# A two-layer decoder trunk on one Trainium2 core: the attention core with stationary values, sparse branches summed in PSUM, and probabilities scaled on VectorE

## The chip, the cores and the metric

The kernel runs on one of the eight cores of one Trainium2 chip. The metric is the device time of one execution in microseconds. Three runs of the kernel before gave 1229.21, 1229.42 and 1230.17 us, so the median is 1229.42 us.

## The reference

The input is one sequence of 256 positions with 1024 channels. Two layers follow each other; the change touches only the attention mixer of the first. Its 8 sparse heads (in 2 groups of 4, which share keys and values) have three branches, each a softmax of its own, combined by sigmoid gates; its 8 "fox" heads have one causal softmax with a bias from a cumulative log forget gate. With 256 positions every block of the selected branch and the whole window are seen, so both are plain causal attention, on their own keys and values.

```python
# sparse heads: three branches per head, each masked_softmax(q k^T * scale) v
o_c = einsum('bgrqn,bngd->bqgrd', p_c, v_cmp)      # 15 compressed blocks
o_s = einsum('bgrqk,bgqkd->bqgrd', p_s, vg)        # selected blocks
o_w = einsum('bgrqk,bkgd->bqgrd', p_w, vw)         # window
o_a = gates[..., 0:1] * o_c + gates[..., 1:2] * o_s + gates[..., 2:3] * o_w
# fox heads
s_f = q k^T * scale + cq[..., None] - cum_t[:, :, None, :]
o_b = einsum('bhqk,bkhd->bqhd', masked_softmax(s_f, causal), vb)
x = x + concatenate([o_a, o_b]) @ w_out
```

After it come a dense SwiGLU, a gated linear attention layer and a mixture of 8 SwiGLU experts. They make up most of the time and are the same in both kernels.

## The kernel before, in words

The program is written by hand, engine by engine: for each engine one function lists its instructions in order, and semaphores (`S["probs"]` and so on) carry what one engine waits for from another. Nothing schedules it: an engine takes its instructions in the written order, and one that waits holds all that stand behind it on that engine.

Weights stream from HBM in units of 1 MB into a ring of eight buffers; ScalarE (ACT in the rows) rounds each unit into a high part (`split`, L1197) and VectorE (DVE) forms the low part (L1577). A product of activations and weights is three matmuls (L562 to L564), high by high, high by low, low by high.

The stage in question stands between the input projection and the output projection. It has 18 units: a unit is one branch (0 selected, 1 window, 2 fox), one tile `t` of 128 queries, and `n` heads, 4 heads with 128 keys each where t is 0, 2 heads with 256 keys each where t is 1. So a unit's scores always fill a PSUM bank of 512 columns. Two units, one of each group of heads, make a pair; there are 9 pairs. For a unit:

1. TensorE (PE) computes the scores of a pair (`qk_pair`, L765) and adds the mask with a matmul against an identity (L768).
2. DVE takes the row maximum from PSUM and multiplies it by minus the scale (`rowmax`, L1830 and L1831).
3. ACT computes the exponentials, head by head, with their row sums (L1327), into `pbuf`, which has two buffers.
4. PE turns the probabilities, four 128x128 transposes (`turn`, L778).
5. DVE copies the turned probabilities from PSUM into `ptb` (L1859).
6. PE multiplies them with the values (`pv`, L796): the turned probabilities are the stationary side (128x128), the values of one head the moving side (64 columns). The result has queries on partitions. Each product of two f32 matrices shows as two matmul records.

After the last unit of each branch and tile DVE runs `take`: reciprocal of the sums (L1838), times the gate (L1843), the product with the branch's output from PSUM (L1844) and the sum into `hn` (L1845), for fox only L1838 and L1840. The compressed branch is one matmul for each tile (L803), its output scaled into `hn` at L1851. The order on PE is: scores of pair p+1, then for both units `turn(u)`, `pv(u-1)`. At the end `hn` is turned for the output projection (L572, 8 transposes for tile 0 before the projection, 8 for tile 1 after its first 12 matmuls), and ACT (L1206) and DVE (L1588) split it into high and low part. Just ahead of the stage DVE does the softmax of the compressed branch (L1805 to L1809), a weight split (L1577) and copies (L1816, L1820).

## Time and profile before

| what | us |
|---|---|
| median of three runs (lowest, highest) | 1229.42 (1229.21, 1230.17) |
| span of the profiled execution, first to last instruction | 1227.6 |
| attention stage in it (first scores to first matmul of the output projection) | 84.72 to 128.17, 43.45 long |
| busy in the whole span: PE, DVE, ACT | 1213.1, 977.8, 815.7 |
| busy in the stage: PE, DVE, ACT | 42.71, 36.55, 22.92 |

The profiled execution has no time of its own in the list beside its span; the median of the runs is 1.8 us above the span. Times in rows are in microseconds from the start of the span; "PEld" is the load of a stationary operand and overlaps the matmuls. A matmul's row says first the stationary shape (contraction * columns), then the output's. The duration of a matmul overlaps the next one's, so that the distance of starts tells its cost.

### The profile page before, as it was taken

Reading aid. Unit: us, or ns where it says so; the run is one execution under the profiler, and the core shown is the slowest. Engines: PE = TensorE matmul, PEld = TensorE weight load, DVE = VectorE, ACT = ScalarE, POOL = GpSimd, SP = SyncE. Lnnn points to the kernel's source line nnn. Section 1 sums busy time; section 2 is a strip of 40 time slices with the busy share of each in tenths; the row PEclk is TensorE's granted clock in tenths of the full one; section 3 lists DMA queues with packets and bytes.
Section 4 is the critical chain, followed back from the end, with each engine's and each line's share of the span. In section 5 each row is a group of like instructions: output and inputs, shape, how many; then the busy total and the mean of one; then the engine's idle time right before and its main releaser. Section 6 shows DMA issues by size and latency. Waiting matters only on the chain.

```text
span 1227.6 us, 16109 instructions
## 1 busy us (share of the span) xinstructions
PE 1213.1 (99%) x5992; PEld 1009.8 (82%) x5992; DVE 977.8 (80%) x959; ACT 815.7 (66%) x877; POOL 35.5 (3%) x41
## 2 busy tenths in 40 slices
PE   8999999999999999999999999999999999999997
PEld 6878888888898888888888888888888888888886
DVE  6998564554557478999989989889889889889896
ACT  7765354344375467777777777777777777777773
POOL 0000000000000001100000000000000000000300
PEclk9999999999999999999999999999999999999999
DMA  9730254455534256999999999999999999999992
GB/s 352 306 137 2 102 192 170 170 188 206 206 138 141 101 192 236 392 397 369 413 367 370 407 370 375 408 365 373 407 368 376 399 372 374 392 364 376 399 421 85
DMA packets 53000, 361.42 MB, mean 294 GB/s; under 512 B 6048, under 2 KB 6560, under 8 KB 10944
## 3 DMA queue, kind: packets, MB, share of 16 engines
q1 hardware_dynamic: 49872, 349.41, 73.8%
q0 software_dynamic: 3056, 11.02, 2.3%
q8 instruction: 50, 0.82, 0.3%
q14 instruction: 22, 0.18, 0.0%
HBM read 354.63 MB, written 5.77 MB: 294 GB/s over the span
## 4 chain that ended last, share of the span: by engine, by line
PE 96%; DVE 1%; ACT 1%; DMA 1%; SPq 0%; issue 0%; DVEq 0%
PE bank L562 29%; PE bank L564 29%; PE bank L563 29%; PE bank L1105 2%; PE bank L796 1%; PE bank L952 1%; PE bank L765 1%; DMA raw<-in_weights 1%; PE bank L572 1%; PE bank L1070 0%; PE bank L778 0%; PE bank L840 0%; ACT hT_hi L1212 0%; PE bank L1062 0%; PE bank L973 0%
## 5 line engine op out<-in xcount | busy, mean ns | idle before, releaser
L2174 DVE TENSOR_TENSOR low<-raw,whi 128x2048 fp32r<-128x2048 f32 x260 | 594.9, 2291 | 66.3 <-ACT whi L1508 59.0
L1508 ACT CAST whi<-raw 128x2048 fp32r<-128x2048 f32 x260 | 497.2, 1912 | 112.3 <-PE bank L564 111.6
L562 PE MATMUL bank<-whi,hT_hi 128*128 128x512 f32 (+1 forms) x1104 | 430.6, 390 | 0.8 <-DVE low L1660 0.5
L564 PE MATMUL bank<-whi,hT_lo 128*128 128x512 f32 (+1 forms) x1104 | 428.7, 388 | 0.0
L563 PE MATMUL bank<-low,hT_hi 128*128 128x512 f32 (+1 forms) x1104 | 428.0, 388 | 0.0
L562 PEld LDWEIGHTS bank<-whi,hT_hi 128*128 128x128 f32 x1104 | 207.4, 188 | 43.4 <-DVE hT_lo L1595 0.9
L564 PEld LDWEIGHTS bank<-whi,hT_lo 128*128 128x128 f32 x1104 | 207.3, 188 | 42.7
L563 PEld LDWEIGHTS bank<-low,hT_hi 128*128 128x128 f32 x1104 | 207.4, 188 | 41.7
L1577 DVE TENSOR_TENSOR low<-raw,whi 128x2048 fp32r<-128x2048 f32 x67 | 152.9, 2288 | 45.0 <-ACT whi L1197 44.9
L562 PE MATMUL bank<-whi,h_hi 128*128 128x512 f32 x440 | 181.0, 411 | 0.0
L564 PE MATMUL bank<-whi,h_lo 128*128 128x512 f32 x440 | 172.5, 392 | 0.0
L563 PE MATMUL bank<-low,h_hi 128*128 128x512 f32 x440 | 172.1, 391 | 0.0
L1197 ACT CAST whi<-raw 128x2048 fp32r<-128x2048 f32 x67 | 128.1, 1918 | 8.2 <-PE bank L564 5.4
L564 PEld LDWEIGHTS bank<-whi,h_lo 128*128 128x128 f32 x440 | 82.6, 188 | 17.9
L563 PEld LDWEIGHTS bank<-low,h_hi 128*128 128x128 f32 x440 | 83.1, 189 | 14.2
L562 PEld LDWEIGHTS bank<-whi,h_hi 128*128 128x128 f32 x440 | 82.7, 188 | 13.7
L1525 ACT ACTIVATE sg<-bank 128x256 f32<-128x256 f32 x88 | 33.9, 385 | 65.2 <-PE bank L564 65.2
L1350 ACT ACTIVATE sg<-bank,rstd 128x256 f32<-128x256 f32 x22 | 10.5, 475 | 98.4 <-PE bank L564 98.3
L1887 DVE SCALAR_TENSOR_TENSOR hact<-bank,rstd,sg 128x256 f32<-128x256 f32 x22 | 10.6, 484 | 57.6 <-ACT sg L1350 57.6
L2179 DVE TENSOR_TENSOR h_lo<-bank,h_hi 128x256 fp32r<-128x256 f32 x88 | 36.8, 418 | 1.0 <-ACT h_hi L1512 1.0
L2191 DVE TENSOR_TENSOR hact<-sg,bank 128x256 f32<-128x256 f32 x88 | 36.4, 414 | 0.0
L1512 ACT CAST h_hi<-bank 128x256 fp32r<-128x256 f32 x88 | 32.8, 373 | 2.8 <-PE bank L1105 2.8
(318 smaller groups left out, 779.4 us busy)
## 6 DMA issues: line engine op xcount, KB each, us to landing
raw<-in_weights SPq DMA_DIRECT2D x327, 1024.0 KB, 5.7
sums<-ybuf POOLq DMA_DIRECT2D x7, 512.0 KB, 6.8
arena<-in_compress SPq DMA_DIRECT2D x1, 1088.0 KB, 15.8
x<-in_x SPq DMA_DIRECT2D x2, 512.0 KB, 5.4
raw<-in_weights SPq DMA_DIRECT2D x4, 256.0 KB, 6.1
raw<-in_weights SPq DMA_DIRECT2D x2, 512.0 KB, 8.0
tokens<-hng POOLq DMA_DIRECT2D x2, 512.0 KB, 8.6
out<-x SPq DMA_DIRECT2D x4, 256.0 KB, 2.7
```

Of the source, the lines that this page charges most:

```text
L562: mm(out_, a_hi, b_hi, start=start, stop=False)
L563: mm(out_, a_hi, b_lo, start=False, stop=False)
L564: return mm(out_, a_lo, b_hi, start=False, stop=stop)
L1105: last = nc.tensor.transpose(bank[2][:, j * P:(j + 1) * P], hact[:, (par + c) % 2, j * P:(j + 1) * P], ident)
L1197: nc.scalar.copy(whi[:, u % SPLIT, :, :], raw[:, u % RAW, :, :]).then_inc(S["w_hi"], 1)
L1508: nc.scalar.copy(whi[:, u % SPLIT, :, :], raw[:, u % RAW, :, :]).then_inc(S["w_hi"], 1)
L1512: nc.scalar.copy(h2_hi[:, (par + c) % 2, :], bank[2][:, 0:CH]).then_inc(S["m_h2_hi"], 1)
L1525: A(sg[:, (par + c) % 2, :], bank[(par + c) % 2][:, 0:CH], ACT.Silu).then_inc(S["m_silu"], 1)
L1577: V.tensor_tensor(low[:, u % RAW, :, :], raw[:, u % RAW, :, :], whi[:, u % SPLIT, :, :].bitcast(F32), ALU.subtract).then_inc(S["w_lo"], 1)
L2174: V.tensor_tensor(low[:, u % RAW, :, :], raw[:, u % RAW, :, :], whi[:, u % SPLIT, :, :].bitcast(F32), ALU.subtract).then_inc(S["w_lo"], 1)
L2179: V.tensor_tensor(h2_lo[:, (par + c) % 2, :], bank[2][:, 0:CH], h2_hi[:, (par + c) % 2, :].bitcast(F32), ALU.subtract).then_inc(S["m_h2T"], 1)
L2191: V.tensor_tensor(hact[:, (par + c) % 2, :], sg[:, (par + c) % 2, :], bank[(par + c) % 2][:, CH:2 * CH], ALU.mult).then_inc(S["m_hact"], 1)
```

## The change

- The values become the stationary side of the product of probabilities and values, and the turned probabilities the moving side: 128x64 stationary, up to 512 moving columns. The output has channels on partitions (64 for each half) and queries along the columns, which is the layout in which the output projection reads it. The two groups of sparse heads (or an even and an odd fox head) write the lower and the upper 64 partitions of the same bank.
- The compressed, selected and window branches of the sparse heads accumulate in one PSUM bank for each tile, so the probabilities must be normalised and gated first: `scaled` on DVE takes the reciprocal of the sums and multiplies each head's probabilities in `pbuf` (now four buffers) by reciprocal and gate, in place, before `turn`.
- `take`, the scaling into `hn`, and the 16 transposes of `hn` are gone. `heads_out` (ACT) and `heads_lower` (DVE) read the output banks directly. The rows of the output weights are permuted on the host (`heads_paired`).
- Queries are stored times minus the scale, masks are +1e30, and the row minimum takes the place of the maximum, so that it is the bias as it stands and L1831 is gone.
- The compressed branch's probabilities are multiplied by their factors before they are turned; its product is four matmuls for each tile.
- The order of pairs and of instructions is another: selected and window of tile 0, then of tile 1, then fox; scores run two pairs ahead.

```diff
+        att_pairs = [(br, 0, 0, 4) for br in range(2)] + [(br, 1, h0, 2) for br in range(2) for h0 in (0, 2)]
+        att_pairs += [(2, 0, 0, 4), (2, 1, 0, 2), (2, 1, 2, 2)]
+        att_units = [(br, t, h0 + 4 * g, n) for br, t, h0, n in att_pairs for g in range(NG)]
...
             def turn(u):
-                pe.wait_ge(S["probs"], u + 1)
+                br, t, h0, n = att_units[u]
+                pe.wait_ge(S["scaled"], u + 1)
...
+            def blocks_out(t):
+                for r in range(4):
+                    c = slice(r * P, (r + 1) * P)
+                    mm(bank[4 + t][:, c], vbd[:, c], pcT[:, t, :], start=(r == 0), stop=False)
+            def pv(p):
+                br, t, h0, n = att_pairs[p]
+                out_ = bank[4 + t]
+                pe.wait_ge(S["probsT"], 2 * p + 2)
+                if br == 2 and h0 == 0:
+                    pe.wait_ge(S["hT"], turned_at(1, t, 0))
+                for kt_ in range(t + 1):
+                    if br < 2:
+                        for g in range(NG):
+                            v = proj[1][:, kt_, br * P + g * HD:br * P + (g + 1) * HD]
+                            last = mm(out_[g * HD:(g + 1) * HD, h0 * P:(h0 + n) * P], v,
+                                      ptb[:, g, kt_ * n * P:(kt_ + 1) * n * P], start=False,
+                                      stop=(br == 1 and h0 + n == 4 and kt_ == t))
+                        continue
+                    for g, j in product(range(NG), range(n)):
+                        h, m = h0 + 4 * g + j, kt_ * n + j
+                        half, c = h % 2 * HD, slice(h // 2 * P, (h // 2 + 1) * P)
+                        last = mm(out_[half:half + HD, c], proj[5][:, kt_, h * HD:(h + 1) * HD],
+                                  ptb[:, g, m * P:(m + 1) * P], start=(kt_ == 0 and h < 2),
+                                  stop=(kt_ == t and h >= 6))
             qk_pair(0)
             pe.wait_ge(S["cmp_pT"], 1)
             for t in range(NT):
-                mm(bank[4 + t][:, :], pcT[:, t, :], vbd, start=True, stop=True).then_inc(S["cmp_o"], 1)
-            for u in range(AU):
-                if u % 2 == 0 and u + 2 < AU:
-                    qk_pair(u + 2)
-                turn(u)
-                if u == AU - 2:
-                    transposes(hn, 1, 0, lambda half: pe.wait_ge(S["o_done"], 7))
-                if u >= 1:
-                    pv(u - 1)
-            pv(AU - 1)
-            by_tile(U_A_OUT, 0, A_OUT_BANKS[0], 1, (0, 4),
-                    lambda: transposes(hn, 1, 1, lambda half: pe.wait_ge(S["o_done"], 8)))
+                blocks_out(t)
+            qk_pair(1)
+            for p in range(AP):
+                turn(2 * p)
+                turn(2 * p + 1)
+                if p + 2 < AP:
+                    qk_pair(p + 2)
+                if p + 1 < AP:
+                    pv(p)
+            by_tile(U_A_OUT, 0, A_OUT_BANKS[0], 1, (0, 4), lambda: pv(AP - 1))
...
-                if u >= 2:
-                    act.wait_ge(S["probsT_psum"], u - 1)
+                if u >= 4:
+                    act.wait_ge(S["probsT_psum"], u - 3)
...
-            V.tensor_tensor(s16, s16, bc(cm01, 2, NH), ALU.mult).then_inc(S["cmp_p"], 1)
+            V.tensor_tensor(s16, s16, bc(cm01, 2, NH), ALU.mult)
...
+            V.tensor_tensor(s16, s16, bc(f3, 3, 16), ALU.mult).then_inc(S["cmp_p"], 1)
             split(14)
...
+            def scaled(u):
+                br, t, h0, n = att_units[u]
+                dve.wait_ge(S["probs"], u + 1)
+                link(V.reciprocal(fac[:, seq_of(u), h0:h0 + n], sums[:, seq_of(u), h0:h0 + n]))
+                kw = (t + 1) * P
+                for h in range(h0, h0 + n):
+                    p_ = pbuf[:, u % 4, (h - h0) * kw:(h - h0 + 1) * kw]
+                    last = V.tensor_scalar(p_, p_, fac[:, seq_of(u), h:h + 1],
+                                           gates[:, t, h, br + 1:br + 2] if br < 2 else 1.0, ALU.mult, ALU.mult)
+                last.then_inc(S["scaled"], 1)
...
+            for u in range(4):
+                row_least(u)
+            scaled(0)
+            scaled(1)
+            for p in range(AP):
+                for u in (2 * p, 2 * p + 1):
+                    probs_turned(u)
+                    if p + 1 < AP:
+                        scaled(u + 2)
+                if p + 2 < AP:
+                    row_least(2 * p + 4)
+                    row_least(2 * p + 5)
+                if p == 3:
+                    heads_lower(0, 0)
+                if p == 6:
+                    heads_lower(1, 0)
+            heads_lower(0, 1)
+            heads_lower(1, 1)
```

Three places show how instructions move. On PE, a pair of tile 1 in the steady part of the stage. Before (bank0 and bank1 take scores, bank2 and bank3 turned probabilities, bank4 and bank5 outputs):

```order
L765 MATMUL bank1<-arena 128x256
L768 MATMUL bank0<-msk_bits 128x2x128
L768 MATMUL bank1<-msk_bits 128x2x128
L778 MATMUL bank2<-cst,arena 128x128 [waits probsT,probs]
L778 MATMUL bank2<-cst,arena 128x128 x3
L796 MATMUL bank4<-arena 128x64 [waits probsT]
L796 MATMUL bank4<-arena 128x64 x3
L778 MATMUL bank3<-cst,arena 128x128 [waits probsT,probs]
L778 MATMUL bank3<-cst,arena 128x128 x3
L796 MATMUL bank5<-arena 128x64 [waits o_done,probsT]
L796 MATMUL bank5<-arena 128x64 x3
```

In the changed kernel (L764 and L767 are scores and mask, L781 the transposes, L802 the product with the values; 64x256 is the output):

```order
L781 MATMUL bank2<-cst,arena 128x128 [waits probsT,scaled]
L781 MATMUL bank2<-cst,arena 128x128 x3
L781 MATMUL bank3<-cst,arena 128x128 [waits probsT,scaled]
L781 MATMUL bank3<-cst,arena 128x128 x3
L764 MATMUL bank6<-arena 128x256 [waits probs]
L764 MATMUL bank7<-arena 128x256
L764 MATMUL bank6<-arena 128x256
L764 MATMUL bank7<-arena 128x256
L767 MATMUL bank6<-msk_bits 128x2x128
L767 MATMUL bank7<-msk_bits 128x2x128
L802 MATMUL bank5<-arena 64x256 [waits probsT]
L802 MATMUL bank5<-arena 64x256 x3
```

Eight products a pair became four, both transposes stand together ahead of the scores, and they wait for `scaled` instead of `probs`.

On DVE, the head of the stage. Before:

```order
L1830 TENSOR_REDUCE arena<-bank0 128x4 [waits scores,dve_chain]
L1831 TENSOR_SCALAR arena<-arena 128x4 [waits dve_chain]
L1830 TENSOR_REDUCE arena<-bank1 128x4 [waits scores]
L1851 TENSOR_TENSOR hn<-bank4,arena 128x512 [waits cmp_o]
L1851 TENSOR_TENSOR hn<-bank5,arena 128x512 [waits cmp_o]
L1830 TENSOR_REDUCE arena<-bank6 128x2 [waits scores]
L1831 TENSOR_SCALAR arena<-arena 128x2 [waits dve_chain]
L1859 COPY arena<-bank2 128x512 [waits probsT_psum]
```

In the changed kernel (L1859 is now the row minimum, L1868 and L1872 are `scaled`, L1881 the copy of turned probabilities):

```order
L1859 TENSOR_REDUCE arena<-bank0 128x4 [waits scores]
L1859 TENSOR_REDUCE arena<-bank1 128x4 [waits scores]
L1859 TENSOR_REDUCE arena<-bank6 128x4 [waits scores]
L1859 TENSOR_REDUCE arena<-bank7 128x4 [waits scores]
L1868 RECIPROCAL arena<-arena 128x4 [waits probs]
L1872 TENSOR_SCALAR arena<-arena 128x128 [waits dve_chain]
L1872 TENSOR_SCALAR arena<-arena 128x128 x3
L1881 COPY arena<-bank2 128x512 [waits probsT_psum]
```

The minima of the second pair now stand ahead of the first scaling, and two scalings ahead of the first copy.

On DVE, one pair of tile 1 in the steady part. Before, with a `take` in it:

```order
L1830 TENSOR_REDUCE arena<-bank0 128x2 [waits scores]
L1831 TENSOR_SCALAR arena<-arena 128x2 [waits dve_chain]
L1859 COPY arena<-bank2 128x512 [waits pv,probsT_psum]
L1838 RECIPROCAL arena<-arena 128x8 [waits pv]
L1843 TENSOR_TENSOR arena<-arena 128x8 [waits dve_chain]
L1844 TENSOR_TENSOR arena<-bank4,arena 128x512 [waits dve_chain]
L1845 TENSOR_TENSOR hn<-hn,arena 128x512 [waits dve_chain]
L1830 TENSOR_REDUCE arena<-bank1 128x2 [waits scores]
L1831 TENSOR_SCALAR arena<-arena 128x2 [waits dve_chain]
L1859 COPY arena<-bank3 128x512 [waits pv,probsT_psum]
```

In the changed kernel:

```order
L1881 COPY arena<-bank2 128x512 [waits pv,probsT_psum]
L1868 RECIPROCAL arena<-arena 128x2 [waits probs]
L1872 TENSOR_SCALAR arena<-arena 128x256 [waits dve_chain]
L1872 TENSOR_SCALAR arena<-arena 128x256
L1881 COPY arena<-bank3 128x512 [waits pv,probsT_psum]
L1868 RECIPROCAL arena<-arena 128x2 [waits probs]
L1872 TENSOR_SCALAR arena<-arena 128x256 [waits dve_chain]
L1872 TENSOR_SCALAR arena<-arena 128x256
L1859 TENSOR_REDUCE arena<-bank6 128x2 [waits scores]
L1859 TENSOR_REDUCE arena<-bank7 128x2 [waits scores]
```

The four instructions of `take`, once for each branch and tile, are gone; a reciprocal and two (tile 0: four) multiplications stand in every unit.

## Rows read from the trace of the kernel before

**Rows 1.** The page: busy time by engine, us (share) and count.

```profile
PE 1213.1 (99%) x5992; PEld 1009.8 (82%) x5992; DVE 977.8 (80%) x959; ACT 815.7 (66%) x877; POOL 35.5 (3%) x41
...
PE 96%; DVE 1%; ACT 1%; DMA 1%; SPq 0%; issue 0%; DVEq 0%
```

**Rows 2.** Busy time by stretch, attention stage: length, engines, granted clock, DMA.

```profile
84.72:128.17 43.45, 42.71 (x344) 36.42 (x343) 36.55 (x79) 22.92 (x100) 0.00 (x0) 1.00 0.06 23
```

**Rows 3.** Groups by form, same stage: count | busy, mean ns | idle before.

```profile
L796 PE MATMUL bank<-arena 128*128 128x64 f32 x144 | 18.9, 274 | 0.7 <-DVE arena L1859 0.6
```

**Rows 4.** Timeline, PE, 104 to 112 us: start, us, engine, line, operation.

```profile
105.14 1.14 PE L765 MATMUL bank<-arena 64*128 64x256 f32 x8
106.20 0.39 PE L768 MATMUL bank<-msk_bits 128*128 128x256 bf16 x2
106.43 0.60 PE L778 MATMUL bank<-cst,arena 128*128 128x128 f32 x4
107.28 1.10 PE L796 MATMUL bank<-arena 128*128 128x64 f32 x8 [0.24 <-DVE arena L1859]
108.22 0.61 PE L778 MATMUL bank<-cst,arena 128*128 128x128 f32 x4
108.68 1.10 PE L796 MATMUL bank<-arena 128*128 128x64 f32 x8
109.62 2.00 PE L765 MATMUL bank<-arena 66*128 66x128 f32 x16
```

**Rows 5.** Timeline, PE, 84.5 to 90 us, the stage's head.

```profile
84.72 1.16 PE L765 MATMUL bank<-arena 64*128 64x128 f32 x16
...
86.39 1.98 PE L803 MATMUL bank<-arena 128*128 128x512 f32 x4
88.30 1.14 PE L765 MATMUL bank<-arena 64*128 64x256 f32 x8
```

**Rows 6.** Timeline, VectorE, 81 to 86.5 us, ahead of the stage.

```profile
81.68 0.42 DVE L1806 TENSOR_TENSOR arena<-arena,cst 128x256 f32<-128x256 f32 x1
82.02 0.24 DVE L1807 RECIPROCAL arena<-arena 128x16 f32<-128x16 f32 x1
82.40 2.29 DVE L1577 TENSOR_TENSOR low<-raw,whi 128x2048 fp32r<-128x2048 f32 x1
84.60 1.40 DVE L1816 TENSOR_SCALAR arena<-bank,sml 66x512 f32<-66x512 f32 x2
85.92 0.41 DVE L1820 COPY arena<-bank 128x256 f32<-128x256 f32 x1
```

**Rows 7.** Timeline, VectorE: copy then row maximum; reciprocal then what is linked to it.

```profile
97.62 0.69 DVE L1859 COPY arena<-bank 128x512 f32<-128x512 f32 x1
98.23 0.68 DVE L1830 TENSOR_REDUCE arena<-bank 128x4 f32<-128x512 f32 x1
...
103.97 0.19 DVE L1838 RECIPROCAL arena<-arena 128x8 f32<-128x8 f32 x1
104.19 0.17 DVE L1843 TENSOR_TENSOR arena<-arena 128x8 f32<-128x8 f32 x1
```

**Rows 8.** Timeline, VectorE, 465 to 494 us: multiplications by one and two columns.

```profile
465.99 0.60 DVE L2109 TENSOR_SCALAR disp<-cst,mtab,rstd 128x128 f32<-128x128 f32 x2
...
492.41 0.87 DVE L2125 TENSOR_SCALAR picks<-cst,mtab 128x128 f32<-128x128 f32 x4
```

**Rows 9.** Groups by form, VectorE, whole span.

```profile
L2109 DVE TENSOR_SCALAR disp<-cst,mtab,rstd 128x128 f32<-128x128 f32 x2 | 0.6, 344 | 0.0
L1646 DVE TENSOR_TENSOR arena<-arena 128x128 f32<-128x128 f32 x1 | 0.3, 295 | 0.0
```

**Rows 10.** Timeline, ScalarE, exponentials of a unit of tile 1.

```profile
97.75 0.48 ACT L1327 ACTIVATE arena<-bank,arena 128x256 f32<-128x256 f32 x1 [2.15 <-DVE arena L1831]
98.12 0.19 ACT L1327 ACTIVATION_READ_ACCUMULATOR arena<-bank,arena 128x1 f32 x1
```

**Rows 11.** Timeline, PE, 38 to 60 us: products with a stationary side of 64 columns.

```profile
41.12 2.06 PE L672 MATMUL bank<-arena 128*64 128x30 f32 x64
```

**Rows 12.** Timeline, PE: eight transposes at the program's start, eight at 131 us.

```profile
4.57 1.97 PE L572 MATMUL bank<-cst,x 128*128 128x128 f32 x8 [4.57 <-DMA cst<-in_constants]
...
131.02 1.03 PE L572 MATMUL bank<-cst,hn 128*128 128x128 f32 x8
```

**Rows 13.** Waits in the stage: who waited for whom, us in total, times, longest.

```profile
ACT arena L1327 <- DVE arena L1831: 18.6, 15, 2.5
DVE arena L1830 <- PE bank L768: 4.4, 4, 1.8
PEld bank L796 <- DVE arena L1859: 1.7, 4, 0.6
```

172 lines of the change are left out of this document (75 added, 97 removed).

## Prediction

> **What bounds the kernel now.** I read the page first. PE is busy 99% of the span and 96% of the chain that ended last is PE [rows 1], so what an engine does elsewhere matters only where PE waits for it. Then the stretch of the attention stage: in its 43.45 us PE is busy 42.71, DVE 36.55, ACT 22.92, at a granted clock of 1.00 [rows 2]. PE bounds this stage too, and DVE is the next, with only 7 us to spare. The waits say the same: ACT waits for DVE (18.6 us in total), DVE for PE (4.4), PE for DVE only 1.7 [rows 13]. Last the timelines, for distances between starts. On PE a pair of tile 1 takes, start to start, 1.29 for scores and mask (105.14 to 106.43), and each of its products with the values about 0.97 (108.68 to 109.62 holds eight records) [rows 4]. The next stage starts when PE reaches the output projection at 128.17, with all its weights there, and from there on PE is again the bound. So the change is worth what it moves that start.
>
> **PE, part by part.** The 144 records of 128x64 [rows 3] stand 0.12 apart, 17.4 us in all. In their place, for a sparse pair of tile 0, stand two products of 512 columns, for tile 1 four of 256, for fox eight of 128: each is two records. No row shows 64 stationary columns with so many moving ones. Nearest below: records on two halves of the contraction rows, which alternate as the new ones do between output halves: eight of 256 columns in 1.14, about 1.06 apart from the next [rows 4, 5]; that form overlaps. Nearest above: records of full height, 0.115 apart at 128 columns (109.62, 16 in 2.00) [rows 4] and 0.49 at most at 512 (four in 1.98) [rows 5], so 1.7 to 1.9 for a pair. The 64 records of the 64-column form stand 0.03 apart at 30 columns [rows 11], a quarter of the 0.12 of the 128-column loads; loads for two halves must overlap there. I take 1.07 for tile 1 and fox, and 1.3 for the two of 512 (the first and last record of four can't overlap: three steps of 0.43). Nine pairs give 2 x 1.3 + 7 x 1.07 = 10.1 instead of 17.4. Eight transposes of `hn` (0.96) leave the stage, and the last product moves behind the first 12 matmuls of the projection, where eight transposes were (1.07 for 0.96). The compressed product stays at 1.9 (16 records of 128 columns at 0.115, for 1.98 [rows 5]). PE's work in the stage falls from about 43 to about 34 us. If PE stayed the bound this would be -9.
>
> It doesn't. **DVE, part by part.** A copy or a row reduction of 512 columns costs 0.60 start to start (97.62 to 98.23) [rows 7]. A reciprocal with something linked to it costs 0.22 [rows 7]. A multiplication of 128 columns by two per-row columns stands 0.256 behind the one before it (0.60 for two, of 0.344 each), by one column 0.195 (0.87 for four) [rows 8, 9]. At 256 columns there is no row. A tensor_tensor of 128 columns takes 0.295 and one of 256 takes 0.42 [rows 9, 6], 0.13 more. A multiplication by two columns costs 0.06 more than by one, so without any it would be about 0.22, less than the 0.295 by half of its 0.13 of streaming; it streams twice as fast, and 128 columns more add 0.067. That is the low end, 0.13 the high; I take the low, since the 128-column rows are of the same operation.
>
> The Trainium skill ("VectorE: DVE Perf Modes", the perf-mode tier table) says that tensor_scalar runs at 2x on fp32 in SBUF and tensor_tensor at 1x. By that rule the low end holds; by the high end the stage would be 1.4 longer (the rival below). The page gives no price for the per-row columns, which here are 0.06 each.
>
> So `scaled` costs 0.22 + 4 x 0.256 = 1.24 for a sparse unit of tile 0, 0.22 + 2 x 0.32 = 0.86 for one of tile 1, 1.0 and 0.74 for fox. A turn of DVE's loop is two copies, two minima and two `scaled`: 2.4 + 2.5 = 4.9 where the next pair is sparse on tile 0, 4.1 on tile 1, 4.4 for fox on tile 0, 3.9 on tile 1. DVE loses L1831 (18 x 0.11), L1851 and `take` (about 12 in all) and gains 17 of scaling: it now has about 41 us in the stage, against PE's 34.
>
> **The walk along DVE.** (1) The compressed softmax has a link and a multiplication of 256 elements more (0.42) [rows 6]: the weight split at 82.40 and all behind it move by 0.46. PE isn't held by the earlier part, since it wants those probabilities only at 84.3. The copy at 85.92 now ends at 86.8, so PE starts the compressed product at 86.8 instead of 86.39 and ends it at 88.7. (2) The scores of pair 1, now four heads of 128 columns, take 1.67 (84.72 to 86.39) [rows 5]: to 90.3. The DVE minima of units 2 and 3 stand ahead of the first scaling, so DVE sits idle from 88.0 to 90.3 though ACT's first exponentials are there at 89. (3) Two minima 1.2, two scalings 2.5: 94.0. PE has nothing from 90.3 to the first transposes at 92.9. (4) Loop turns: 4.9 to 98.9; three of 4.1 and one split of `heads_lower` (0.6) to 111.9; 4.1 to 116.1; 4.4 and a wait of 0.45 to 120.9 (four exponentials of fox unit 12 take ACT 1.5 behind their minimum, DVE has 1.2 of other work for it; at two heads, 0.46 each [rows 10], they are in time); 3.9 and 0.6 to 125.4; the last without minima 2.7 to 128.1. Small waits, 0.03 each, add 0.2: 128.3. (5) PE, which runs ahead of DVE by 0.3 to 1 us in each turn (its pair is 1.25 + 0.96 + 1.07 = 3.3), has pair 7's product at 127.6 to 128.6, then the last eight transposes, 0.96: the projection starts at 129.6, for 128.17 before: +1.4. (6) In the projection +0.1. The lower halves for its second four row blocks come from `heads_lower(0, 1)` behind the last copies, at about 131, wanted at 133.5; those of tile 1 at 134.8, wanted at 139. Weight split 15 stands behind pair 8's product as it stood behind the transposes. Nothing is late.
>
> Costed at nothing: queries copied with a scale (0.07 more on ACT, which has over 20 us to spare in the stage), one instead of two steps for the minima (counted), the other output banks. All later stages are bound by PE and hold the same instructions; a shift at 129 us passes through to the end.
>
> **Sum:** +1.5. The profiled execution's span was 1227.6; 1229.1 for its like, and with the 1.8 by which the median of the runs stands above that span, 1230.9.
>
> **The rivals.** (A) *The two output halves do not overlap on PE*; slower. Then a sparse pair's products take 1.75 and fox 1.9. A turn of DVE's loop holds: second copy ready at 0.60 + 0.86 + 0.69 = 2.15, then product, then transposes up to the next copy, 0.7. With 1.75 this is 4.65, over 4.1; it decides from 1.25 of product on. Over the tile-1 and fox turns that is 5 x 0.5, and 0.9 in front of the last transposes: +3.3 more, 1234.2. For it: no row with overlapping matmuls on output halves; the 0.03 of rows 11 could be overlapping loads alone. Against it: the row halves overlap in this trace [rows 4].
>
> The Trainium skill says in "TensorEngine Tiling (Array Packing)", Key Properties, that tiles run loads and matmuls in parallel, but that a change of tiling mode drains TensorE. Scores, mask, transposes and products change it four times a pair. By the first half A is false; by the second PE loses a little of its 0.3 to 1 us of slack in each turn. The rows have such changes too (scores to mask to transposes) and show 0.1 to 0.2 for one, inside the distances that I used.
>
> (B) *PE's clock falls in the new waits*; slower. After 4.57 us of waiting at the program's start eight transposes took 1.97, with a busy PE 1.03 [rows 12]: the lower of two levels, 1.2 for 2.4 GHz. In the stage before, the granted clock is 1.00 throughout and no wait of PE for DVE exceeds 0.6 us [rows 2, 13]. Now there are two waits of about 2.5 us (90.3 and 125) and PE works three quarters of the time. If the clock is low for two pairs, PE's 3.3 become 6.6 against DVE's 4.1: +5, 1236. Nothing in the trace says whether 2.5 us is enough.
>
> The Trainium skill ("TensorE: Matmul & The Clock Gate", the HAM clock gate) says that idle time lets the clock fall to 1.2 GHz and that transposes don't count as busy the same way, which speaks for B. The start of this trace agrees on the first point.
>
> (C) *Wide multiplications stream once per cycle*: 8 sparse units of tile 1 and 4 of fox, two each, 0.065 more: +1.5, 1232.4.
>
> (D) *DVE isn't the bound*; faster. If PE's 34 us went straight through behind the first wait, the projection would start at 84.7 + 34 + 3.2 = 122 to 124: 1225. Against it stands the DVE sum, whose terms all have rows but one.
>
> **How the numbers follow.** A change of 0.2% (2.5 us) is about what a measurement of this kernel can tell from none. Forecast case 0.60 (own range 1229.5 to 1232.5), A 0.17, B 0.10, C 0.07, D 0.06. Slower by over 0.2% means over 1231.9: A, B, most of C and 0.07 of the forecast case, 0.38. Faster means under 1227.0: D and a little, 0.07. The rest, 0.55, is no change. The range goes from 1228.7 to 1235.5: it leaves out D and most of B.
>
> **What would show it.** DVE without idle time from 91 to 128 us but for 0.45 once, and PE idle for about 11 us in the stage, most of it waiting for `scaled` (L1872) or copies; a first wait of PE of about 2.6 us; L1872 at 0.41 for 256 columns; products of a sparse pair of tile 1 in about 1.2; the projection's first matmul at 129.6; a clock of 1.00. A product of 1.75 shows A, transposes of twice the length B, 0.48 for L1872 C. I am wrong if DVE has idle time inside the loop, or if the stages behind change length.

## The result and the profile after

The changed kernel takes 1236.39 us (median of 19 executions, 1231.82 to 1243.83), the kernel before 1230.74 beside it (19, 1229.21 to 1234.19): ratio 1.0049, 95% interval 1.0036 to 1.0063. It is slower by 5.7 us; 1230.9 was forecast, and the range ended at 1235.5. The profiled execution took 1234.12 with a span of 1232.3, 4.7 more than the span of before. One execution of the kernel before in a slow state (1457.56 us, a mean granted clock of 0.784) is left out of everything below.

The page of the changed kernel: busy time by engine, and the chain that ended last [rows 1].

```profile
PE 1209.3 (98%) x5932; PEld 1000.0 (81%) x5932; DVE 980.9 (80%) x986; ACT 814.9 (66%) x877; POOL 35.6 (3%) x41
...
PE 89%; DVE 7%; issue 1%; ACT 1%; DMA 1%; SPq 1%; DVEq 0%
```

DVE stood for 1% of the chain and now stands for 7%: the attention stage hangs on it. The stage from its first scores to the first matmul of the output projection, as in [rows 2] (length, PE, PE's loads, DVE, ACT, POOL, granted clock, DMA share, GB/s), and two stretches in it and one at the router:

```profile
84.73:130.65 45.92, 37.58 (x275) 26.00 (x275) 40.26 (x107) 22.73 (x101) 0.00 (x0) 0.93 0.05 21
...
94.00:98.00 4.00, 3.83 (x16) 2.23 (x18) 3.93 (x14) 0.00 (x0) 0.00 (x0) 0.59 0.00 0
102.00:124.00 22.00, 19.78 (x150) 13.84 (x146) 21.26 (x57) 11.59 (x50) 0.00 (x0) 1.00 0.00 1
128.00:132.00 4.00, 4.00 (x24) 3.48 (x21) 1.87 (x4) 0.00 (x0) 0.00 (x0) 0.57 0.00 0
...
465.00:470.00 5.00, 5.00 (x27) 3.50 (x27) 2.36 (x16) 3.07 (x3) 0.79 (x2) 0.66 0.21 90
```

43.45 us became 45.92, PE's work in it fell from 42.71 to 37.58, and the granted clock, 1.00 throughout before, is 0.93. While the engines work, the low clock sits in three places: about 94.0 to 97.4, about 127.9 to 131.3, and about 466 to 469.3. (It is low once more from about 1230.5 on, behind the last instruction of every engine, where it costs nothing; before has such a stretch too.)

PE at the stage's head and its end (start, us, engine, line, operation, in brackets the idle time before and who ended it), the counterpart of [rows 5] and the last line of [rows 12]:

```profile
84.73 1.16 PE L764 MATMUL bank<-arena 64*128 64x128 f32 x16
...
89.93 0.61 PE L767 MATMUL bank<-msk_bits 128*128 128x512 bf16 x2
92.94 0.66 PE L781 MATMUL bank<-cst,arena 128*128 128x128 f32 x4 [2.40 <-DVE arena L1872]
94.17 1.11 PE L781 MATMUL bank<-cst,arena 128*128 128x128 f32 x4 [0.58 <-DVE arena L1872]
95.21 2.08 PE L764 MATMUL bank<-arena 64*128 64x256 f32 x8
...
127.55 1.55 PE L809 MATMUL bank<-arena 128*64 128x128 f32 x16 [2.32 <-DVE arena L1881]
129.03 1.97 PE L781 MATMUL bank<-cst,arena 128*128 128x128 f32 x8
130.65 0.78 PE L561 MATMUL bank<-whi,hT_hi 128*128 128x512 f32 x1
```

Two waits, 2.40 and 2.32 us, and work of twice the usual length behind each: eight score records 2.08 instead of 1.14 [rows 4], eight transposes 1.97 instead of 1.03 [rows 12]. Between them PE is ahead of DVE in every turn:

```profile
105.54 1.08 PE L802 MATMUL bank<-arena 128*64 128x256 f32 x8 [0.59 <-DVE arena L1881]
106.56 1.09 PE L781 MATMUL bank<-cst,arena 128*128 128x128 f32 x8
107.58 1.14 PE L764 MATMUL bank<-arena 64*128 64x256 f32 x8
```

DVE at the head and over one turn of its loop [rows 7 and 8]:

```profile
90.36 1.29 DVE L1859 TENSOR_REDUCE arena<-bank 128x4 f32<-128x512 f32 x2 [2.36 <-PE bank L767]
91.56 0.17 DVE L1868 RECIPROCAL arena<-arena 128x4 f32<-128x4 f32 x1
91.77 1.11 DVE L1872 TENSOR_SCALAR arena<-arena 128x128 f32<-128x128 f32 x4
...
103.37 0.68 DVE L1881 COPY arena<-bank 128x512 f32<-128x512 f32 x1
103.97 0.15 DVE L1868 RECIPROCAL arena<-arena 128x2 f32<-128x2 f32 x1
104.15 0.73 DVE L1872 TENSOR_SCALAR arena<-arena 128x256 f32<-128x256 f32 x2
104.80 0.68 DVE L1881 COPY arena<-bank 128x512 f32<-128x512 f32 x1
105.40 0.15 DVE L1868 RECIPROCAL arena<-arena 128x2 f32<-128x2 f32 x1
105.60 0.73 DVE L1872 TENSOR_SCALAR arena<-arena 128x256 f32<-128x256 f32 x2
106.25 1.28 DVE L1859 TENSOR_REDUCE arena<-bank 128x2 f32<-128x512 f32 x2
107.45 0.68 DVE L1881 COPY arena<-bank 128x512 f32<-128x512 f32 x1
```

The turn from 103.37 to 107.45 is 4.08; 4.1 was forecast. DVE has no idle time in it.

The 4.7 us between the two profiles, place by place: the output projection starts 2.5 later (128.17 to 130.65), where 1.4 was forecast; the first product of the router 3.2 later (458.30 to 461.53); the first dispatch behind it 4.4 later (466.74 to 471.13). Each step up is a place with a low clock. At the router its mark is six idle matmuls (products whose result nobody reads) in 2.72, in the profile of before 1.45:

```profile
462.80 1.45 PE L584 MATMUL bank<-msk_bits 128*128 128x512 bf16 x6
...
466.13 2.72 PE L583 MATMUL bank<-msk_bits 128*128 128x512 bf16 x6
```

These steps are not the clock alone. The experiments have three profiles of the changed loop at a clock of 1.00 throughout the stage; it is 44.3 long in each. This one has no idle matmuls in it ("halves apart" below):

```profile
85.18:129.49 44.31, 35.02 (x275) 24.21 (x275) 39.87 (x107) 22.70 (x101) 0.00 (x0) 1.00 0.05 22
```

So of the 2.5 us by which the stage grew, 0.9 (43.45 to 44.31) is the changed work and 1.6 (44.31 to 45.92) the low clock. In the projection 0.7 is added, of which 0.3 is there at a clock of 1.00 too (profile of "both waits filled"). The router adds 1.2, the end of the program 0.3.

### The profile page after: what moved, and what is told of

Read it like the earlier page. It is cut to its first block, busy times and chain, and to the rows that moved or that the text cites. A ratio compares the mean times of both kernels' runs of the same rounds, so it can differ in the third digit from the quotient of the medians.

```text
span 1232.3 us, 16009 instructions
## 1 busy us (share of the span) xinstructions
PE 1209.3 (98%) x5932; PEld 1000.0 (81%) x5932; DVE 980.9 (80%) x986; ACT 814.9 (66%) x877; POOL 35.6 (3%) x41
## 4 chain that ended last, share of the span: by engine, by line
PE 89%; DVE 7%; issue 1%; ACT 1%; DMA 1%; SPq 1%; DVEq 0%
PE bank L561 27%; PE bank L563 27%; PE bank L562 27%; PE bank L1117 2%; DVE low L1604 1%; DMA raw<-in_weights 1%; PE bank L964 1%; DVE arena L1872 1%; DVE arena L1881 1%; DVE arena L1859 1%; PE bank L1082 0%; PE bank L571 0%; PE bank L852 0%; PE bank L781 0%; PE bank L583 0%
## 5 line engine op out<-in xcount | busy, mean ns | idle before, releaser
L1604 DVE TENSOR_TENSOR low<-raw,whi 128x2048 fp32r<-128x2048 f32 x67 | 152.9, 2288 | 45.0 <-ACT whi L1209 44.9
```

The source lines that it names most:

```text
L1604: V.tensor_tensor(low[:, u % RAW, :, :], raw[:, u % RAW, :, :], whi[:, u % SPLIT, :, :].bitcast(F32), ALU.subtract).then_inc(S["w_lo"], 1)
```

## The experiments

Each was measured beside the kernel before. "Clock" is the mean granted clock over all executions, and "at 0.998" how many of them had 0.998 or more over their whole length, with their mean time. Executions of the kernel before had 0.9973 in the first group, with 17 of 30 at 0.998 or more (1230.1). "Start" is that of the output projection in the profiled execution, before 128.17. The stage itself begins anywhere from 84.1 to 85.6 in these profiles, so the text gives its length where tenths matter. The mean clock covers the end of the program too, where no engine works, so that it is a rough measure: two profiles with a mean of 0.998 differ by a whole low stretch of 3.4 us at the router.

| kernel | median (executions) | ratio, 95% interval | clock | at 0.998 | start |
|---|---|---|---|---|---|
| first wait filled | 1233.42 (12) | 1.0023, 1.0011 to 1.0035 | 0.9962 | 3, 1232.0 | 129.80 |
| last wait filled | 1233.56 (12) | 1.0014, 1.0002 to 1.0026 | 0.9962 | 5, 1231.6 | 129.55 |
| both waits filled | 1233.74 (12) | 1.0016, 1.0003 to 1.0030 | 0.9961 | 2, 1230.5 | 128.93 |
| scaling early | 1236.23 (7) | 1.0055, 1.0034 to 1.0077 | 0.9929 | 0 | 129.41 |
| changed kernel again | 1237.53 (5) | 1.0051, 1.0026 to 1.0075 | 0.9922 | 0 | 130.94 |
| copies on ACT | 1240.36 (6) | 1.0069, 1.0048 to 1.0089 | 0.9913 | 0 | 129.48 |
| copies on ACT, early | 1235.18 (12) | 1.0036, 1.0020 to 1.0052 | 0.9926 | 0 | 127.91 |
| no scaling | 1231.05 (10) | 0.9995, 0.9973 to 1.0016 | 0.9951 | 2, 1224.7 | 122.65 |
| before, with a wait | 1237.03 (5) | 1.0044, 1.0023 to 1.0064 | 0.9948 | 0 | 133.36 |
| before, wait filled | 1234.10 (10) | 1.0024, 1.0010 to 1.0038 | 0.9970 | 5, 1232.7 | 130.67 |
| halves apart | 1241.82 (7) | 1.0076, 1.0052 to 1.0100 | 0.9924 | 0 | 129.49 |
| both filled, router too | 1231.86 (10) | 1.0005, 0.9993 to 1.0017 | 0.9987 | 9, 1231.9 | 128.77 |
| before, router filled | 1230.16 (10) | 0.9997, 0.9987 to 1.0007 | 0.9984 | 9, 1230.2 | 127.55 |
| rebalanced | 1228.09 (10) | 0.9987, 0.9969 to 1.0005 | 0.9968 | 4, 1226.7 | 123.84 |
| rebalanced, filled | 1229.17 (12) | 0.9985, 0.9972 to 0.9997 | 0.9965 | 5, 1226.7 | 123.98 |
| the same, router too | 1227.93 (12) | 0.9976, 0.9966 to 0.9986 | 0.9977 | 7, 1227.4 | 124.12 |

**The two waits filled.** Ten idle matmuls of 128x512 in each wait, or in one:

```diff
             for p in range(AP):
+                if p == 0:                          # first wait
+                    pe.wait_ge(S["foxT_late"], 2)
+                    keep_busy(10, 3)
                 turn(2 * p)
...
+                if p == 7:                          # last wait
+                    pe.wait_ge(S["probs"], 16)
+                    keep_busy(10, 6)
                 if p + 1 < AP:
                     pv(p)
```

> Ten idle-time matmuls (bf16, 128x512, 0.22 us each) fill TensorE's first long wait (90.5 to 92.9 us), where it waits for the first scaled probabilities. Theory 1 (the long waits let the clock fall): no fall behind 92.9, the low stretch of 3.4 us at 94 us is gone and the time falls by 1 us or more against the changed kernel; the fall at the stage's end (128 us) stays. Rival 2 (what counts is that TensorE works only three quarters of the whole stage): the fall only moves to another place in the stage, and the time stays near 1236. Rival 3 (the missing 5 us are in later stages, nothing to do with the clock in this one): the low stretch goes but the time does not follow.

> Ten such matmuls fill the last long wait (125.2 to 127.6 us), ahead of the product of pair 7. Theory 1: the low stretch at 128 us is gone, the output projection starts about 1.0 us earlier (129.6 for 130.65) and its first matmuls run at the upper level; the fall at 94 us stays. Rival 2: a fall shows elsewhere. Rival 3: no change of time.

> Both fillings. Theory 1: granted clock in the stage 1.00, output projection at 129.6, median near 1231 to 1232 and little scatter between executions (the changed kernel's spread was 12 us). Rival 2: falls remain in the middle of the stage, clocks of executions still 0.990 to 0.995, median over 1234. Rival 3: median 1235 or more with a clock of 1.00 in the stage.

With the first wait filled the profile has a clock of 1.00 from 90 to 124 and 0.79 from 124 to 132; with the last filled, 0.83 from 90 to 100 and 1.00 from 100 to 132; with both, 1.00 in all of the stage. Each fill takes away the low clock behind its own wait and leaves the other. So the clock falls behind the wait, and not because of the lighter load of the loop, which is the same in all three. The stage is 45.92 long with both waits empty, 45.52 with the first filled, 44.80 with the last filled and 44.30 with both: the low clock behind the first wait costs some 0.5 us, that behind the last 1.2. With both filled the projection starts at 128.93, under the 129.6 of the forecast. The medians fall by 2.7 to 3.0 us, alike for all three, so they do not follow these lengths, and both filled misses the 1231 to 1232 that was expected. Most executions still have low stretches, in the profile of both filled at the router (0.89 from 460 to 475).

**Scaling earlier, and the changed kernel again.**

```diff
-            for u in range(4):
-                row_least(u)
+            row_least(0)
+            row_least(1)
             scaled(0)
+            row_least(2)
+            row_least(3)
             scaled(1)
```

> VectorE scales unit 0 ahead of the minima of units 2 and 3. By my walk its wait shrinks from 2.4 to about 1 us and all behind it, the output projection too, comes 1.2 us earlier; TensorE's first wait shrinks from 2.4 to about 0.5 us, so by theory 1 the fall at 94 us goes too: 2 to 3 us less than the changed kernel. If the clock has nothing to do with the wait: 1.2 us less and the same falls.

> The changed kernel once more, for another execution's trace. Theory 1 (the clock falls behind the two long waits): low stretches of 3.4 us near 94 and 128 us of this or a neighbouring position, or only one of them, by chance of where they fall. Theory 2 (three-quarter load is enough anywhere in the stage): a low stretch in the middle of the stage (98 to 124 us) in slow executions.

The early scaling lets the first transposes start at 90.42, splits the first wait and leaves 1.93 of it; no low clock follows (1.00 from 90 to 124). The last wait stays at 2.31 with the low clock behind it, and the median doesn't move: 1236.23. That misses the wait of 0.5 and the 2 to 3 us that were expected. The second profile of the changed kernel repeats the first: waits of 2.40 and 2.32, clocks of 0.57 from 94 to 98 and from 128 to 132, 0.66 from 465 to 470.

It shows one thing more. This execution took 1241.55 us and the first 1234.12, yet DVE's last instructions stand within 0.3 us of each other:

```profile
1224.67 2.47 DVE L2209 TENSOR_TENSOR x<-x,bank 128x512 f32<-128x512 f32 x4
...
1224.96 2.47 DVE L2209 TENSOR_TENSOR x<-x,bank 128x512 f32<-128x512 f32 x4
```

DVE, the last engine at work, is done at 1227.14 and 1227.43; the spans end at 1232.3 and 1239.7. So 7.1 of the 7.4 us between two executions of the same kernel lie behind all computation, after 5.2 us in one and 12.3 in the other. In the longer one the queue of instructions still moves four packets behind 1231, in the shorter one none. The mean clock of the longer one is lower (0.992 for 0.995) by the low clock of this end alone: both have the same three low stretches of 3.4 us before it. In all other profiles the end is 4.7 to 6.5 long. Of the changed kernel's executions 11 of 24 took over 1238 us (9 of 19 and 2 of 5); of those with a wait filled none of 46 did, of the kernel before none. Only one of the executions over 1238 has a trace, so whether the others owe it to the end of the program is not shown, nor what lengthens it. But the fills took these executions away, and they change the program as well as the clock, so that the fall of the medians is no measure of the low clock alone. Without the executions over 1238 the median of the first 19 is 1234.1, and 1233.74 with both waits filled.

**DVE relieved.** In the first two kernels ACT makes the 18 copies of turned probabilities, in the second with the early scaling (of this edit the line alone is shown; each pair's copies stand ahead of the exponentials of the pair two further on, and tile 1's first half is split one pair earlier). In the third the multiplications shrink to one of 8 columns for each unit, so the probabilities stay unnormalised.

```diff
-                V.tensor_copy(ptb[:, u % 2, :], bank[2 + u % 2][:, :]).then_inc(S["probsT"], 1)
+                nc.scalar.copy(ptb[:, u % 2, :], bank[2 + u % 2][:, :]).then_inc(S["probsT"], 1)
```

```diff
-                for h in range(h0, h0 + n):
-                    p_ = pbuf[:, u % 4, (h - h0) * kw:(h - h0 + 1) * kw]
+                for h in range(h0, h0 + 1):
+                    p_ = pbuf[:, u % 4, 0:8]
```

> ScalarE, busy 21 of 45 us in the stage, takes the 18 copies of turned probabilities (0.59 each) from VectorE. VectorE's turn for a sparse pair of tile 1 falls from 4.1 to 2.9 us, ScalarE's rises from 1.8 to 3.0, TensorE's is 3.3: TensorE bounds the loop. If the walk along VectorE was right, the projection starts about 6 us earlier than with the changed kernel (near 123 us), and with TensorE busy the clock stays: median 1225 to 1227, faster than before by 0.3%. If copies were not the bound: no change of the stage.

> The same, with unit 0 scaled ahead of the minima of units 2 and 3, and unit 1 behind them. The first wait of TensorE shrinks, since VectorE's wait of 2.4 us moves behind the first scaling: 1 us less than the copies on ScalarE alone, and fewer falls of the clock.

> The multiplications of the probabilities are left out but for one of 8 columns in each unit (the probabilities stay unnormalised), 12 us of VectorE's work. By the walk VectorE's turn falls to 3.1 us for a sparse pair of tile 1, under TensorE's 3.3: the projection starts 7 to 8 us earlier, at about 122 us, and VectorE waits for TensorE again. If VectorE's sum were not the bound, it would start near 129.6 as now.

Without the multiplications the projection starts at 122.65, 8.0 earlier than in the changed kernel's profile, with waits of 1.57 and 1.35 and a clock of 1.00 in the stage: DVE's scaling is what the stage waits for. Like for like, at a clock of 1.00, the stage is 37.74 long instead of 44.31. The median does not show it: executions lie from 1223.66 to 1235.45, and the profiled one has the low clock for 10 us at the router. The copies on ACT missed what was expected by far: the projection at 129.48 for 123, and a median of 1240.36 for 1225 to 1227; with the early scaling 127.91 and 1235.18. PE idle before a group, in the run with early scaling:

```profile
PE bank L802 <- ACT arena L1356: 2.1, 2, 1.6
PE bank L809 <- ACT arena L1356: 2.0, 1, 2.0
PE bank L781 <- DVE arena L1884: 1.9, 1, 1.9
```

The copies stand behind a pair's exponentials and behind the split of the finished heads on ACT, and PE waits for them: 1.65 us at 115.55, 2.04 at 125.33. A low stretch follows each (0.57 from 116 to 120, 0.61 from 126 to 128). Without the early scaling a wait of 1.66 at 118.70 has none behind it. The loop was relieved of DVE's load and got new long waits instead.

**A wait put into the kernel before.** This one tells the clock apart from everything else of the change.

```diff
+                for _ in range(4 if u == 0 else 0):
+                    link(V.tensor_copy(ptb[:, 0, :], bank[2][:, :]))
                 V.tensor_copy(ptb[:, u % 2, :], bank[2 + u % 2][:, :]).then_inc(S["probsT"], 1)
```

```diff
+                if u == 1:
+                    keep_busy(12, SCORE_BANKS[0][0])     # only in the second kernel
                 if u >= 1:
                     pv(u - 1)
```

> The kernel BEFORE the change, with one thing added: VectorE makes the first copy of turned probabilities four times more than needed (four times 0.6 to 0.75 us with its link), which lengthens TensorE's wait ahead of its first product with the values from 0.38 us (rows of before) to about 3.1. Nothing else of the change is in it. Theory 1 (a wait of TensorE of that length, at this place, is what brings the low clock): +2.7 to 3.0 from the wait and a low stretch of 3.4 us behind it, which costs another 1.5 to 2: the output projection begins at 132.3 to 133.2 instead of 128.17, median +4 to +5 against before. Rival (the falls belong to the changed loop's lower load or to its form of matmuls, and a single wait does nothing): clock 1.00 through the stage, output projection at 130.9 to 131.2, median +2.7 to +3.

> The same kernel before the change with the same four extra copies, and in the wait that they make TensorE runs twelve idle 128x512 bf16 matmuls of about 0.21 us each. Theory 1: the wait is filled, no low stretch behind it, the output projection at 130.9 to 131.3, and the median 1.5 to 2 us below that of the run without the idle matmuls. Rival: the same time as without them, within 0.3 us.

PE behind the added wait without the fill, and with it:

```profile
93.93 1.97 PE L796 MATMUL bank<-arena 128*128 128x64 f32 x8 [3.28 <-DVE arena L1861]
95.83 2.08 PE L765 MATMUL bank<-arena 64*128 64x256 f32 x8
97.84 0.61 PE L768 MATMUL bank<-msk_bits 128*128 128x256 bf16 x2
```

```profile
90.64 2.75 PE L584 MATMUL bank<-msk_bits 128*128 128x512 bf16 x12
94.08 1.10 PE L796 MATMUL bank<-arena 128*128 128x64 f32 x8 [0.69 <-DVE arena L1863]
95.12 1.13 PE L765 MATMUL bank<-arena 64*128 64x256 f32 x8
```

The products start at the same time and take 1.97 and 1.10. The granted clock from 94 to 102:

```profile
94.00:102.00 8.00, 8.00 (x46) 6.94 (x48) 4.09 (x10) 2.04 (x8) 0.00 (x0) 0.62 0.00 0
```

```profile
94.00:102.00 8.00, 7.91 (x71) 6.84 (x71) 6.68 (x17) 3.06 (x12) 0.00 (x0) 1.00 0.00 0
```

The projection starts at 133.36 and 130.67, and the medians are 1237.03 and 1234.10 (5 and 10 executions; the intervals of the two ratios overlap, so the 2.7 us between the starts is the firmer number). The low clock cost 2.7 to 2.9 us in a kernel that has nothing of the change in it; here it lasted some 6.8 us in the profile (0.90 from 90 to 94, 0.62 from 94 to 102), so the 1.5 to 2 of the expectation were too few. The wait by itself cost 2.7, as expected.

**Output halves issued apart.**

```diff
-                for kt_ in range(t + 1):
-                    if br < 2:
-                        for g in range(NG):
+                if br < 2:
+                    for g, kt_ in product(range(NG), range(t + 1)):
```

> The changed kernel with the products of sparse pairs at the second query tile issued by output half (both key tiles of one group, then both of the other) instead of alternating between the halves. Prediction's first rival (halves that don't run beside each other): in the changed kernel's profile eight products of 256 columns in two halves took 1.08 us like four of 512. Theory 1 (neighbouring matmuls into different halves run beside each other, those into the same half don't): the eight records now take 1.5 to 1.7 us, four pairs of them; TensorE waits for VectorE in the loop, so the output projection moves by less than 0.5 us and the time stays at the changed kernel's within 1 us. Rival (the order of issue does not matter for the overlap): 1.08 us as before.

Eight records with the two key tiles of one half behind each other:

```profile
105.61 1.09 PE L801 MATMUL bank<-arena 128*64 128x256 f32 x8 [0.59 <-DVE arena L1882]
109.69 1.09 PE L801 MATMUL bank<-arena 128*64 128x256 f32 x8 [0.58 <-DVE arena L1882]
```

1.09, for 1.08 in the changed kernel: theory 1 falls, the order of issue makes no difference. This profile also shows that the low clock is a matter of chance: behind a wait of 2.40 at 93.38 and one of 2.32 at 127.62 the clock stayed at 1.00 through the stage, and the projection started at 129.49, where 129.6 was forecast (its stage began at 85.18, 0.45 late, so the stage itself is 0.6 shorter than forecast). The median of its seven executions, 1241.82, lies above the changed kernel's, since five of the seven took over 1238 us. PE's and DVE's rows agree with those of the changed kernel to 0.02; the long end of the program seen above is the likeliest reason, but the profiled execution (1234.71) has an end of 6.0, so it stays open.

**How often a wait brings the low clock.** Over the profiles of all versions of the changed kernel, TensorE has twelve empty waits of 2.0 to 2.4 us in the stage, and a low stretch follows ten (the two without are in the profile just shown). Of the eight empty waits of 1.3 to 1.93 us one has a low stretch behind it. Of the six waits of the first kind that were filled with ten idle matmuls none has.

**The router.** Two idle matmuls instead of one behind each of the first three groups of eight-column products, five instead of six behind the last, in the changed kernel with both waits filled and in the kernel before:

```diff
-            keep_busy(1, 5)
+            keep_busy(2, 5)
             logits(0, 1)
...
-            keep_busy(6, 5)
+            keep_busy(5, 5)
```

> The changed kernel with both long waits of the attention stage filled with ten idle matmuls (as in the earlier run with both filled), and besides, at the router (457 to 466 us), two idle 128x512 bf16 matmuls instead of one behind each of the first three groups of eight-column products, five instead of six behind the last: two more in all. Theory 1 (what is left of the loss is the low stretch at the router, which comes after a run of products of only eight columns): fewer executions with a granted clock under 0.998, median 1231 to 1232.5 instead of 1233.7. Rival (the router's low stretch has another cause, such as the load over a longer time): the same spread as before, median 1233.5 to 1234.5, by 0.4 later for the added matmuls.

> The kernel BEFORE the change with the same two more idle matmuls at the router and nothing else. Theory 1: its executions with a low stretch at the router (over half of them so far, 1232 to 1234) become few, its median falls from about 1231 to 1230 or just under. Rival: no fewer low stretches, median +0 to +0.5.

Nine of ten executions of each are at 0.998 or more, for 2 of 12 and 18 of 34 without. The medians fall to 1231.86 (from 1233.74) and 1230.16 (from 1231.16; this smaller fall is within its noise, ratio 0.9997, 0.9987 to 1.0007). The added matmuls are not free. The product behind them starts at 464.49 in both profiles of before, but the router began at 458.30 without them and at 457.65 with them: 6.19 against 6.84, and 6.84 in the changed kernel too (459.65 to 466.49). The three that were added stand ahead of the last group of eight-column products, which starts 4.35 behind the first instead of 3.70, and DVE waits for that group. Nor do they always keep the clock up. The changed kernel's profile still has a low stretch of 3.4 us, from about 467.5, at a mean clock of 0.998:

```profile
465.00:470.00 5.00, 4.55 (x22) 2.88 (x21) 3.78 (x22) 1.21 (x2) 0.00 (x0) 0.75 0.00 0
```

These two kernels compare the change with less low clock on either side: +1.7 us between the medians.

**The loop shared out anew.** ACT makes 15 of the 18 copies, DVE those of units 10, 11 and 17; the split of finished heads stands ahead of the exponentials; scaling is early. The other two add eight idle matmuls in the first wait and five in the last, and then the router's.

```diff
+                if p != 5:
+                    probs_turned(2 * p)              # on ACT
+                if p not in (5, 8):
+                    probs_turned(2 * p + 1)
                 if p == 3:
                     heads_out(0, 0)
-                if p == 7:
+                if p == 6:
                     heads_out(1, 0)
+                if p + 2 < AP:
+                    exponentials(2 * p + 4)
+                    exponentials(2 * p + 5)
```

> The changed kernel with the work of the loop shared out anew: ScalarE copies 15 of the 18 units of turned probabilities, VectorE three (the two of the sixth pair, which came late behind eight narrow exponentials, and the very last); the split of the finished output halves stands ahead of the exponentials of its pair instead of behind; and the first multiplications stand ahead of the third and fourth row minima. Theory 1 (VectorE bounds the changed loop, and each long wait of TensorE costs the wait and then a fall of the clock): the row minima, multiplications and three copies are some 30 us of VectorE in a stage of 43; in the run with copies on ScalarE and the early multiplications the output projection began at 127.91 with two falls of 3.4 us in the stage and waits of 1.65 and 2.04; both waits shrink by about 1.5, and the falls that followed them go if the waits were their cause: output projection at 123.5 to 126, executions without a fall at 1226 to 1228, median 1227 to 1231. Theory 2 (the falls come from the loop's lower load in general, whatever its waits): two or more falls stay in the stage, output projection at 126.5 or later, median 1232 to 1235.

> The changed kernel with the loop's work shared out anew (as in the run 'rebalanced': median 1228.1, output projection at 123.84, waits of 1.93 at the head and 1.30 before the eighth pair's product) and eight idle matmuls in the first of these waits (between the first pair's two units of transposes) and five in the second. Theory 1 (a wait of about 2 us brings the low clock in some executions, and a filled one in none): output projection at 123.8 to 124.3, fewer executions under a mean granted clock of 0.998, median 1226.5 to 1228, below the kernel before by 2.5 to 4 us. Rival (the low clocks that rebalanced still had, in six of ten executions, are all at the router): median as before, 1228 to 1228.5.

> The same, with two more idle matmuls at the router as well. Theory 1 for the router (few eight-column products in a row bring the low clock there): nearly all executions at 0.998 or more, median 1226 to 1227. Rival: as without them, plus 0 to 0.5.

The stage of the last of them, and PE's waits in it:

```profile
84.60:123.90 39.30, 37.11 (x284) 25.11 (x286) 32.48 (x92) 29.13 (x114) 0.00 (x0) 1.00 0.06 25
```

```profile
PE bank L809 <- ACT arena L1362: 0.7, 2, 0.5
PE bank L802 <- ACT arena L1362: 0.4, 1, 0.4
PE bank L789 <- DVE arena L1874: 0.4, 1, 0.4
PE bank L781 <- DVE arena L1892: 0.2, 1, 0.2
```

DVE has 32.5 us of work instead of 40.3 and ACT 29.1 instead of 22.7; the projection starts at 124.12, 4.0 before that of the kernel before. The last version is faster than the kernel before: 1227.93 against 1231.16, ratio 0.9976 (0.9966 to 0.9986). Part of that is the router's fill; against the kernel before with the same fill (1230.16) 2.2 us are left. Filling the waits alone did nothing here (1229.17 against 1228.09, with five of 12 executions at 0.998 or more): the profile of the version without fills shows a clock of 1.00 in the stage and at the router already, so no trace shows where its slower executions lose their time. The router's fill on top brought 7 of 12 to 0.998 or more and missed the "nearly all" and the 1226 to 1227 that were expected.

## Why the prediction was wrong

**The step that failed is the clock.** The sum took the stage at a granted clock of 1.00 ("a clock of 1.00" stands among the signs), and set the fall aside as rival B with 0.10. It said itself that nothing in the trace of before tells whether 2.5 us of waiting is enough. It is, in most traces: ten of twelve such waits have a low stretch behind them, the filled ones none, and the wait added to the kernel before brought one too. The sign that was named for B, transposes of twice the length, is there (1.97). So the low clock, put at nothing in the sum, cost 1.6 us in the stage and about 0.4 in the projection. A second term put at nothing was everything behind: "a shift at 129 us passes through to the end". The router, with the same instructions, took 1.2 longer in the profile at a low clock, and the end of the program can take 7 more. B was also put in the wrong place. It was priced for two pairs in the middle of the stage; the clock was 1.00 there (102 to 124 in the profile) and low behind the first wait, behind the last and at the router. A low stretch behind the first wait costs little (0.5), since PE has slack behind DVE there; the one at the end (1.2) falls on the last product, the last transposes and the projection, where all is on the path. That B's 1236 is near the median is a coincidence.

The Trainium skill ("TensorE: Matmul & The Clock Gate", The HAM clock gate) says that the throttled clock is the default and that activity releases it. The runs agree for most waits: 0.50 behind an empty one, 1.00 behind the same wait with idle matmuls in it; two empty ones of 2.40 and 2.32 had 1.00 behind them as well. What the prediction says of transposes stands on the same page under "Part 4: PE-mode transpose"; no run here tests it.

**Where the time went.** In the pair of profiles 4.7 us are: changed work in the stage 0.9 and in the projection 0.3, low clock in the stage 1.6, in the projection 0.4 and at the router 1.2, the end of the program 0.3. So about 1.2 is the change itself and over 3 the clock. The 5.7 us between the medians can't be split in this way. The kernel before has low stretches at the router in some executions as well, and 9 of the changed kernel's 19 are over 1238 us, the kind whose one trace has the long end and no more low clock before it than the faster one. Why such executions come with the changed kernel is open.

**The walk along DVE held, with some luck at its end.** The copy ended at 86.8 as forecast; DVE's minima began at 90.36 (90.3); PE's first wait ended at 92.94 (92.9); the turns took 4.08 (4.1); the product of pair 7 started at 127.55 (127.6). But 127.55 holds some delay by the low clock, and the 129.49 of the profile without a fall belongs to a stage that began 0.45 late. At a clock of 1.00 the stage is 44.3 long, where the walk had 44.9 (84.7 to 129.6): +0.9 for +1.4. DVE's work in it is 39.9, where about 41 was added up. The projection adds 0.3 for 0.1, so the change itself comes to +1.2 there for +1.5, and to +1.7 in the medians with both waits and the router filled.

**Sizes.** Multiplications of 256 columns stand 0.325 apart (two from 104.15 to the copy at 104.80), as the low end had it: rival C is false. The products of a pair of tile 0 took 1.08 at a clock of 1.00 and not 1.3 (profile of the first wait filled); the 1.07 of the others was right. In a stage that DVE bounds this moved nothing. PE's work of 34 us in the stage was right too: at a clock of 1.00 it is 35.02, and 34.18 without the multiplications. In rival A the turn of 2.15, 1.75 and 0.7 adds up to 4.60, not 4.65, which changes nothing.

```profile
96.16 1.08 PE L802 MATMUL bank<-arena 128*64 128x512 f32 x4 [0.39 <-DVE arena L1884]
```

**Rivals A and D.** A (halves that don't overlap) is false: 1.08 for a pair. But its reason in the prediction, that neighbours in different halves are what makes it short, is not confirmed either: issued apart, they took 1.09. D (DVE isn't the bound) is false: without the multiplications the stage shrank to 37.74.

## What to carry to other kernels

When a change takes work from TensorE and gives it to another engine, count the waits that TensorE gets and look how long each is: here a wait added to the kernel before cost 2.7 us by itself and 2.9 by the low clock behind it. Put idle matmuls into such a wait in one version before judging the change, and look at the granted clock of several executions, not of one. Keep in mind that a fill is work too (0.65 us at the router), and that a mean clock also counts the end of the program. Where executions of one kernel differ by more than the clock can explain, take a second trace and compare where the last instruction ends. Then share the added work out: the 8.5 us that PE saves became a gain of 3.2 (2.2 against the kernel before with the same fill at the router) only once ACT and DVE were both under PE's time.

## What the runs showed of the hardware

- Twelve empty waits of TensorE of 2.0 to 2.4 us in a stage at full clock: a granted clock of 0.5 for 3.4 us behind ten, none behind two. One of 3.28: 6.8 us. Of eight from 1.30 to 1.93 one (1.65) had a low stretch behind it. Filled with idle matmuls, six of the first kind and the one in the kernel before: none.
- At the router the clock fell with PE shown as busy throughout (5.00 of 5.00 us from 465 to 470), behind groups of eight-column products, for 3.4 us (the changed kernel), 6.8 (halves apart) or 10.2 (scaling early). One more idle matmul behind each of three groups, and one less at the end, brought the share of executions at 0.998 or more from 18 of 34 to 9 of 10 in the kernel before, for 0.65 us of added time; one trace with it still has a low stretch.
- Products with 64 stationary columns took 0.27 for each record of 512 columns and 0.135 of 256, against 0.49 for 512 with 128 stationary columns [rows 5]; at 256 columns the order of the halves made no difference.
- A multiplication of 256 columns of fp32 by two per-row columns stands 0.325 behind the one before, 0.256 at 128 columns [rows 8].
- Behind the last instruction of any engine a span went on for 4.7 to 6.5 us in 17 profiles and for 12.3 in one, with four packets on the queue of instructions in its last 9 us.
